# One more weight chunk under the projection, x ahead of the weights, and the last 8 MB in another order

## The chip, the cores and the metric

The kernel runs on one core of a Trainium2 chip. The metric is the device time in microseconds of one execution. Before the change it is 1363.29 us, the median of three runs (1362.73 to 1363.33).

## The reference

One layer on x, 256 rows of 2048 float32:

```
h    = rms_norm(x) ; proj = h @ w_in                    # 2048 x 6736
x   += [sparse attention || retention](proj) @ w_out    # 2048 x 2048
h    = rms_norm(x)
top group of 4, then the top 2 of its 8 experts, gates from a softmax
y    = sum over experts of  gate * ( silu(h @ w1[e]) * (h @ w3[e]) ) @ w2[e]
out  = x + y                                            # w1, w3: 32 x 2048 x 512, w2: 32 x 512 x 2048
```

The attention takes the 64 best keys of a block-causal index score; the retention is a decayed product of queries and keys with a rotation in front. w_in and w_out are 72 MB together, the expert weights 32 x 12 MB, which is 384 MB. Every expert weight is read once.

## The kernel before, in words

**Projection stage.** `w_in` and `w_out` come in 72 loads of up to 1 MB (index `q`) into four raw buffers (`RAW`). Each load holds two units (index `u`, 144 in all); ACT rounds a unit into `w_hi` (L574), DVE takes the rest into `w_lo` (L854), and PE multiplies three times (L1304 to L1306), 12 products of 128x512 to a unit. `SPLIT` is 4: ACT may be four units ahead of PE. At the beginning PE transposes x (`turn_x`, L1266), part by part as its four 512 KB column parts land, and ACT and DVE split the result in two (`round_z`, `rest_z`). PE's program holds all eight `turn_x` before the first unit, and the attention, the retention and the router are put between units at fixed places of each engine's program.

**SyncE's queue.** SP issues in program order x part 0, the identity, the first gain, raw load 0, x parts 1 to 3, then the raw loads. From `q` = 4 on a raw load waits until DVE has finished the units four loads back (`lo_done`). Beside the raw loads 65 to 68 it issues four chunks of expert weights, and after the last raw load the others, as their places come free.

**GpSimd's queue.** It issues the small constants (four gain vectors, the retention gains, the table of positions and cosines) once x is transposed, and, once the retention is done (`ret_ready`), the second norm's gains and the router's weights, seven small transfers. Its own work is the q and k gains, the rotation, and copies of x.

**Expert stage.** Experts go in eight teams of four. A team has 24 chunks of 2 MB: 16 of w1 and w3, 8 of w2 (`TEAM_CHUNKS`). The ring holds `RING` = 8 chunks of 16 KB a partition. The first team has `EXTRA` = 3 more places: the x buffer, once its content is copied away (chunk 8), and two over the buffers of the projection (`spare`, chunks 9 and 10). `first_slot(k)` gives the slot of the first team's chunk k, `first_landed` and `chunk_landed` what to wait for. SP loads chunk k when `ring_used` says that its slot is free; later teams fetch w1 and w3 in loads of 4 MB. PE gathers a team's tokens (L1514), multiplies up (L1559), turns the hidden rows, multiplies down (L1597) and scatters (L1526) into x, where DVE adds. Between the last router logits and the first gather PE waits for the choice of experts (`sel_ready`), which DVE makes.

**The end.** The last team's second half of w2 (rows s = 0 and 1 of each partition, 2048 columns each) comes in three `LAST_PIECES`, each of four transfers (one an expert): row 0 whole (4 MB), row 1's column blocks 0 and 1 (2 MB), row 1's blocks 2 and 3 (2 MB). After each of the two last pieces PE multiplies its blocks (L1649), ACT copies them (L816), PE scatters them (L1661), DVE adds them to x (L1238), and SP stores the output in three parts (L461).

The software DMAs of GpSimd have a reservation of 16 KB a partition in SBUF.

Of the kernel before, what the change touches and what calls it, by code (L numbers as in the profile page):

```python
# [36 lines left out]
P = 128  # L37
SEQ, D = 256, 2048
TH = SEQ // P
C = D // P  # L40
CHUNK = 64
HEADS, HD, KV = 8, 128, 2
# [9 lines left out]
NB = 512  # L52
# [23 lines left out]

RING, EXTRA = 8, 3
UP_CHUNKS, DOWN_CHUNKS = 4 * TEAM, 2 * TEAM
TEAM_CHUNKS = UP_CHUNKS + DOWN_CHUNKS
LAST_GROUP = TEAM_CHUNKS - TEAM  # L80
LAST_PIECES = [(0, 0, 4), (1, 0, 2), (1, 2, 2)]
STORES = [(0, 2), (2, 1), (3, 1)]
# [16 lines left out]
def chunk_slot(k):  # L99

    return k % RING
# [22 lines left out]
def build(nc, x, norm1_g, w_in, q_norm_g, k_norm_g, idx_k_ln_w, idx_k_ln_b, ret_norm_g, w_out,  # L124
          norm2_g, w_group, w_router, w1, w3, w2, consts, out):
    ctx = ExitStack()
    with ctx:
        def sb(name, shape, dt=F32):
            return ctx.enter_context(nc.sbuf_tensor(name, shape, dt))

        def sem(name):
            return ctx.enter_context(nc.semaphore(name))
# [34 lines left out]
        g2_col = sb("g2_col", [P, C])  # L167
        g2_gate = sb("g2_gate", [P, C])
        ps = ctx.enter_context(nc.psum_tensor("ps", [P, 8, 512], F32))

# [10 lines left out]
        xs_flat = xs[:, :, :].rearrange("p t n -> p (t n)")  # L181
        extra = [xs_flat, spare[0], spare[1]]
        zT = half_buf[:, :].rearrange("p (b c t) -> p b c t", b=2, c=4)
# [90 lines left out]
        stored = sem("stored")  # L274
        ring_used = sem("ring_used")
        raw_landed = [sem(f"raw_landed{i}") for i in range(RAW)]
        hi_done, lo_done = sem("hi_done"), sem("lo_done")
# [95 lines left out]
        def _(sp):  # L373
# [36 lines left out]
            for q in range(UNITS // 2):  # L410
                if q == 1:
                    for i in range(1, X_PARTS):
                        load_x(i)
                if q >= RAW:
                    sp.wait_ge(lo_done, 2 * (q - RAW) + 2)
                at = raw_buf[:, q % RAW * 2048:(q % RAW + 1) * 2048]
                if 2 * q >= UNITS_IN:
                    nb, e = OUT_ORDER[2 * q - UNITS_IN]
                    src, c, col, n = w_out_v, 2 * e, nb * NB, NB
                else:  # L420
                    col, n = block_cols(q // 4)
                    src, c = w_in_v, q % 4 * 4
                sp.dma_start(at[:, 0:4 * n].rearrange("p (c n) -> p c n", c=4),
                             src[:, c:c + 4, col:col + n]).then_inc(raw_landed[q % RAW], 16)
# [18 lines left out]
            def last_team(it):  # L443

                matrices(it, TEAMS - 1)
                for k in range(UP_CHUNKS, LAST_GROUP):
                    sp.wait_ge(ring_used, it * TEAM_CHUNKS + (k - RING + 1))
                    load(k, TEAMS - 1)
                for i, (j, n, count) in enumerate(LAST_PIECES):
                    at = j * D + n * NB  # L450
                    for m in range(TEAM):
                        k = LAST_GROUP + m
                        if i == 0:
                            sp.wait_ge(ring_used, it * TEAM_CHUNKS + (k - RING + 1))
                        src = w2_v[(TEAMS - 1) * TEAM + m, 1]
                        sp.dma_start(ring[:, chunk_slot(k), at:at + count * NB],
                                     src[:, at:at + count * NB]).then_inc(piece_in[i], 16)
                for n, count in STORES:
                    sp.wait_ge(added, it * 8 + (16 + TH * (n + count)))
                    cols = slice(n * NB, (n + count) * NB)  # L460
                    sp.dma_start(out_t[:, :, cols], xs[:, :, cols]).then_inc(stored, 16)  # L461

# [35 lines left out]
        def _(pool):  # L498
            pool.wait_ge(z_turned, 8)
            for dst, src in ((gain_q, q_norm_g), (gain_k, k_norm_g), (ln_w, idx_k_ln_w), (ln_b, idx_k_ln_b)):  # L500
                pool.dma_start(dst, src.partition_broadcast(P).rearrange("p l n -> p (l n)")).then_inc(gains_in, 16)
            pool.dma_start(gr_rows[:, :], ret_norm_g.rearrange("l (h d) -> (l h) d", d=HD)).then_inc(ret_gain_in, 16)
            pool.dma_start(const[:, P:CONSTS], consts[:, P:CONSTS]).then_inc(const_in, 16)
            pool.wait_ge(gains_in, 64)
# [8 lines left out]
            for part, blocks in ((RQ, 8), (RK, 10)):  # L513
                pool.wait_ge(evacuated, 2 * blocks)
                for th in range(TH):
# [11 lines left out]
                    pool.wait_ge(rotated, n)  # L527
            pool.wait_ge(ret_ready, 2)
            pool.dma_start(g2_col[:, :], norm2_g.rearrange("l (p c) -> p (l c)", c=C)).then_inc(g2_in, 16)
            pool.dma_start(g2_gate[:, :].rearrange("p (q c) -> p q c", q=4),  # L530
                           norm2_g.rearrange("l (q p c) -> p (l q) c", q=4, c=4)).then_inc(g2_in, 16)
            pool.dma_start(stage_g.rearrange("p (q n) -> p q n", q=4), w_group.rearrange("l (q p c) g -> p (l q) (c g)", q=4, c=4)).then_inc(router_in, 16)
            for g in range(GROUPS):
                pool.dma_start(stage_r[:, g].rearrange("p (q n) -> p q n", q=4),
                               w_router[0, g].rearrange("(q p c) e -> p q (c e)", q=4, c=4)).then_inc(router_in, 16)
            for nb in range(OUT_BLOCKS):
# [11 lines left out]
        def _(act):  # L548
# [21 lines left out]
            def round_unit(u):  # L570
                act.wait_ge(raw_landed[u // 2 % RAW], 16 * (u // 2 // RAW + 1))
# [259 lines left out]
        def _(v):  # L831
# [183 lines left out]
            def router_weights():  # L1015
# [13 lines left out]
                last.then_inc(router_laid, 1)  # L1029

            for u in range(UNITS):
                if u < 8:
                    rest_z(u)
                rest_unit(u)
# [220 lines left out]
        def _(pe):  # L1255
# [379 lines left out]
            def last_team(it):  # L1635
                ups(it)
                pe.wait_ge(added, it * 8 + 16)
                turn_hm(it)
                turn_gate(it)
                pe.wait_ge(hm_T_ready, it + 1)  # L1640
                down(it, (0,))
                pe.wait_ge(gate_T_ready, it + 2)
                for i, (j, n0, count) in enumerate(LAST_PIECES):
                    pe.wait_ge(piece_in[i], 16 * TEAM)
                    for n in range(n0, n0 + count):
                        for m in range(TEAM):
                            part = slice(SLOTS * m, SLOTS * (m + 1))
                            at = j * D + n * NB
                            last = mm(ps[part, 4 + n, :], hm_lhsT(m, 2 + j),  # L1649
                                      ring[:, chunk_slot(LAST_GROUP + m), at:at + NB], start=False, stop=(j == 1))  # L1650
                        if j == 1:
                            last.then_inc(y_whole, 1)
                    if j == 0:
                        continue
                    for n in range(n0, n0 + count):
                        pe.wait_ge(y_ready, it * 4 + (4 + n + 1))
                        for th in range(TH):
                            s = TH * n + th
                            if s >= 2:
                                pe.wait_ge(added, it * 8 + (16 + s - 1))  # L1660
                            mm(ps[:, 3 - s % 2, :], gate_T[:, th * P:(th + 1) * P], y_sb[:, n * NB:(n + 1) * NB],  # L1661
                               start=True, stop=True).then_inc(scattered, 1)

# [49 lines left out]
```

## Time and profile before

| what | value |
|---|---|
| median of three runs | 1363.29 us |
| profiled execution, its own time | 1364.37 us |
| its span | 1362.5 us |
| mean granted TensorE clock | 0.865 |
| PE / DVE / ACT / POOL busy | 72% / 24% / 23% / 6% of the span |
| moved by the DMA engines | 480.69 MB, mean 353 GB/s |

Times inside the profile are microseconds from the start of the span. PE is the matrix engine, PEld its weight load, SPq the issue of DMAs by SP, L and a number a line of the kernel. A row of the timeline has a start, a duration, the engine, the line, the operation and how many are merged. An fp32 product shows as two records.

### The profile page before, as it was taken

To read this page: it belongs to the slowest core of one execution; us is meant where nothing else is said; L and a number is where in the kernel's file an instruction comes from. 1 tells how busy PE (TensorE), PEld (TensorE's weight loads), DVE (VectorE), ACT (ScalarE), POOL (GpSimd) and SP (SyncE) were. 2 spreads that over 40 slices of the span, in tenths; PEclk is the share of its full clock that TensorE was granted. 3 is DMA by queue.
4 is the path that set the end of the run, shared out by engine and by line. 5 is a ranking of instruction groups with operands and counts; after the bars stand their busy time and mean duration, and the time that the engine had idled before them with its cause. 6 is when DMAs were issued, how large, how long until landed. Compare 5 with 4: busy or idle time off the path is not lost.

```text
span 1362.5 us, 18965 instructions
## 1 busy us (share of the span) xinstructions
PE 985.4 (72%) x8264; PEld 654.3 (48%) x8264; DVE 330.6 (24%) x504; ACT 306.6 (23%) x553; POOL 80.0 (6%) x61
## 2 busy tenths in 40 slices
PE   7999999999999875556566365547736563674547
PEld 6987887888888651324234133313413421342222
DVE  5457967544753200010010000001001000100101
ACT  6545555555543310001001000100100010010000
POOL 1000242500110020000000000000000000000000
PEclk9999999999999888778787777888878777986888
DMA  8744644544596999999999999999999999999997
GB/s 278 231 153 158 213 145 137 183 164 147 192 411 237 405 426 435 430 426 431 432 432 425 436 431 427 433 431 433 424 435 432 426 434 432 429 425 435 430 423 305
DMA packets 61412, 480.69 MB, mean 353 GB/s; under 512 B 3816, under 2 KB 8096, under 8 KB 43952
## 3 DMA queue, kind: packets, MB, share of 16 engines
q1 hardware_dynamic: 60832, 478.89, 85.9%
q0 software_dynamic: 528, 1.06, 0.3%
q8 instruction: 38, 0.62, 0.2%
q14 instruction: 14, 0.11, 0.0%
HBM read 477.84 MB, written 2.10 MB: 352 GB/s over the span
## 4 chain that ended last, share of the span: by engine, by line
DMA 48%; PE 47%; DVE 2%; SPq 1%; issue 1%; ACT 1%; ACTq 0%
DMA ring<-w_dram 48%; PE ps L1559 11%; PE ps L1304 9%; PE ps L1306 9%; PE ps L1305 9%; PE ps L1597 5%; DVE w_lo L854 1%; PE ps L1514 1%; PE ps L1320 1%; DMA xs<-x_dram 1%; SPq L393 1%; PE ps L1661 1%; PE ps L1414 0%; PE ps L1336 0%; SPq L400 0%
## 5 line engine op out<-in xcount | busy, mean ns | idle before, releaser
L1559 PE MATMUL ps<-ring,side_buf 128*32 128x256 f32 x4000 | 273.5, 438 | 252.3 <-DMA ring<-w_dram 252.3
L1559 PEld LDWEIGHTS ps<-ring,side_buf 128*32 128x32 f32 x4000 | 155.9, 126 | 372.9 <-issue 316.1
L1304 PE MATMUL ps<-w_hi,zT_half 128*128 128x512 f32 (+2 forms) x576 | 221.7, 385 | 1.7 <-DVE w_lo L854 1.7
L1306 PE MATMUL ps<-w_hi,zT_half 128*128 128x512 f32 (+2 forms) x576 | 218.6, 379 | 0.0
L1305 PE MATMUL ps<-w_lo,zT_half 128*128 128x512 f32 (+2 forms) x576 | 218.5, 379 | 0.0
L854 DVE TENSOR_TENSOR w_lo<-raw_buf,w_hi 128x1024 fp32r<-128x1024 f32 (+2 forms) x144 | 182.0, 1281 | 142.7 <-ACT w_hi L574 142.0
L1597 PE MATMUL ps<-ring,side_buf 128*32 128x512 f32 x960 | 129.6, 701 | 97.5 <-DMA ring<-w_dram 97.2
L574 ACT CAST w_hi<-raw_buf 128x1024 fp32r<-128x1024 f32 (+2 forms) x144 | 143.6, 1016 | 107.5 <-PE ps L1306 101.4
L1230 DVE TENSOR_TENSOR xs<-xs,ps 128x512 f32<-128x512 f32 x56 | 38.5, 688 | 487.8 <-PE ps L1526 487.7
L792 ACT ACTIVATE side_buf<-ps,st 128x256 f32<-128x256 f32 x16 | 6.7, 470 | 554.2 <-PE ps L1559 554.2
L1597 PEld LDWEIGHTS ps<-ring,side_buf 128*32 128x32 f32 x960 | 35.8, 127 | 186.0 <-issue 179.5
L1304 PEld LDWEIGHTS ps<-w_hi,zT_half 128*128 128x128 f32 x576 | 108.2, 188 | 23.3 <-DVE w_lo L854 3.2
L1306 PEld LDWEIGHTS ps<-w_hi,zT_half 128*128 128x128 f32 x576 | 108.1, 188 | 20.5
L1305 PEld LDWEIGHTS ps<-w_lo,zT_half 128*128 128x128 f32 x576 | 108.2, 188 | 19.2
L1218 DVE SCALAR_TENSOR_TENSOR side_buf<-ps,st,side_buf 128x256 f32<-128x256 f32 x16 | 7.0, 479 | 253.4 <-ACT side_buf L792 253.4
L1514 PE MATMUL ps<-const,buf_a 128*128 128x128 f32 x512 | 63.6, 284 | 0.0
L1514 PEld LDWEIGHTS ps<-const,buf_a 128*128 128x128 f32 x512 | 60.4, 197 | 3.6 <-issue 3.3
L809 ACT COPY side_buf<-ps 128x512 f32<-128x512 f32 x28 | 14.4, 600 | 207.2 <-PE ps L1597 207.2
L1526 PE MATMUL ps<-side_buf 128*128 128x512 f32 x112 | 54.0, 618 | 0.0
L765 ACT ACTIVATE side_buf<-ps,g_col 128x128 f32<-128x128 f32 x128 | 36.5, 368 | 36.2 <-PE ps L1514 36.2
L1526 PEld LDWEIGHTS ps<-side_buf 128*128 128x128 f32 x112 | 17.3, 188 | 33.8 <-DVE xs L1230 27.5
L1206 DVE TENSOR_TENSOR const<-route,const 128x256 f32 (+1 forms) x8 | 3.4, 424 | 60.8 <-PE ps L1585 59.9
(192 smaller groups left out, 501.3 us busy)
## 6 DMA issues: line engine op xcount, KB each, us to landing
ring<-w_dram SPq DMA_DIRECT2D x56, 4096.0 KB, 25.1
ring<-w_dram SPq DMA_DIRECT2D x73, 2048.0 KB, 21.4
raw_buf<-w_in_dram SPq DMA_DIRECT2D x48, 1024.0 KB, 5.0
raw_buf<-w_out_dram SPq DMA_DIRECT2D x16, 1024.0 KB, 6.0
spare<-w_dram SPq DMA_DIRECT2D x2, 2048.0 KB, 13.1
ring<-w_dram SPq DMA_DIRECT2D x4, 1024.0 KB, 14.0
ring<-w_dram SPq DMA_DIRECT2D x8, 512.0 KB, 17.4
raw_buf<-w_in_dram SPq DMA_DIRECT2D x4, 608.0 KB, 6.2
```

The lines of the kernel that those rows point to most:

```text
L574: nc.scalar.copy(split(w_hi, u), raw(u)).then_inc(hi_done, 1)
L765: last = nc.scalar.activation(h_e[:, c, :], ps[:, 2 + j % 2, cc * P:(cc + 1) * P], ACT.Copy, scale=g2_col[:, c:c + 1])
L809: nc.scalar.copy(y_sb[:, n * NB:(n + 1) * NB], ps[:, 4 + n, :]).then_inc(y_ready, 1)
L854: V.tensor_tensor(split(w_lo, u), raw(u), split(w_hi, u).bitcast(F32), ALU.subtract).then_inc(lo_done, 1)
L1230: V.tensor_tensor(xo, xo, ps[:, 3 - s % 2, :], ALU.add).then_inc(added, 1)
L1304: mm(b, zhi(c)[:, t], wh, start=(c == 0), stop=False)
L1305: mm(b, zhi(c)[:, t], wl, start=False, stop=False)
L1306: last = mm(b, zlo(c)[:, t], wh, start=False, stop=(c == C - 1))
L1514: last = mm(ps[:, 2 + j % 2, (c % 4) * P:(c % 4 + 1) * P], z[:, th, c * P:(c + 1) * P], pick_p[:, th].rearrange("p e s -> p (e s)"), start ...
L1526: mm(ps[:, 3 - s % 2, :], gate_T[:, th * P:(th + 1) * P], y_sb[:, n * NB:(n + 1) * NB], start=True, stop=True).then_inc(scattered, 1)
L1559: last = mm(ps[part, up, pair * WIDE:(pair + 1) * WIDE], h_e[:, c, slots], w[m][:, cc * NB + h * WIDE:cc * NB + (h + 1) * WIDE], start=(c ...
L1597: last = mm(ps[part, 4 + n, :], hm_lhsT(m, j), w[m][:, j % 2 * D + n * NB:j % 2 * D + (n + 1) * NB], start=(j == 0), stop=(j == J - 1))
```

## The change

`EXTRA` becomes 4. The fourth place is a new buffer `place` of 16 KB a partition; the software DMAs' reservation is set to 128 bytes. The first team's chunk 11 goes there, issued by SP ahead of raw load 40. With `EXTRA` the slots of the first team turn by one: beside the raw loads 65 to 68 go the chunks 4 to 7, afterwards 0, 2, 1 and 3 (before: 5, 6, 7, 0, then 1, 3, 2 and 4).

All transfers that GpSimd issued are SP's: the six constants ahead of raw load 5, and the seven of the router ahead of raw load 63, behind a wait for `ret_ready`. At the start SP issues x parts 1 and 2, then raw load 0's first half with a semaphore of its own, x part 3, and raw load 0's second half. ACT and DVE take their part of x one unit earlier. PE gets three products of 128x512 into an unused bank ahead of the wait for `sel_ready`. The last pieces are: both rows of the column blocks 0 and 1 (4 MB), row 0 of blocks 2 and 3 (2 MB), row 1 of them (2 MB); PE scatters the blocks 0 and 1 after the first piece and the blocks 2 and 3 after the last.

```diff
-RING, EXTRA = 8, 3
+RING, EXTRA = 8, 4
-LAST_PIECES = [(0, 0, 4), (1, 0, 2), (1, 2, 2)]
+LAST_PIECES = [(0, 2, 0, 2), (0, 1, 2, 2), (1, 1, 2, 2)]
+        place = sb("place", [P, 4096])
-        extra = [xs_flat, spare[0], spare[1]]
+        extra = [xs_flat, spare[0], spare[1], place[:, :]]
@@ sync: in the loop over the raw loads q
-                if q == 1:
-                    for i in range(1, X_PARTS):
-                        load_x(i)
+                if q == 5:
+                    for dst, src in ((gain_q, q_norm_g), (gain_k, k_norm_g), (ln_w, idx_k_ln_w), (ln_b, idx_k_ln_b)):
+                        sp.dma_start(dst, src.partition_broadcast(P).rearrange("p l n -> p (l n)")).then_inc(gains_in, 16)
+                    sp.dma_start(gr_rows[:, :], ret_norm_g.rearrange("l (h d) -> (l h) d", d=HD)).then_inc(ret_gain_in, 16)
+                    sp.dma_start(const[:, P:CONSTS], consts[:, P:CONSTS]).then_inc(const_in, 16)
+                if q == 40:
+                    load_first(11)
+                if q == 63:
+                    sp.wait_ge(ret_ready, 2)
+                    sp.dma_start(g2_col[:, :], norm2_g.rearrange("l (p c) -> p (l c)", c=C)).then_inc(g2_in, 16)
+                    sp.dma_start(g2_gate[:, :].rearrange("p (q c) -> p q c", q=4),
+                                 norm2_g.rearrange("l (q p c) -> p (l q) c", q=4, c=4)).then_inc(g2_in, 16)
+                    sp.dma_start(stage_g.rearrange("p (q n) -> p q n", q=4),
+                                 w_group.rearrange("l (q p c) g -> p (l q) (c g)", q=4, c=4)).then_inc(router_in, 16)
+                    for g in range(GROUPS):
+                        sp.dma_start(stage_r[:, g].rearrange("p (q n) -> p q n", q=4),
+                                     w_router[0, g].rearrange("(q p c) e -> p q (c e)", q=4, c=4)).then_inc(router_in, 16)
...
+                if q == 0:
+                    load_x(1)
+                    load_x(2)
+                    sp.dma_start(at[:, 0:2 * n].rearrange("p (c n) -> p c n", c=2),
+                                 src[:, c:c + 2, col:col + n]).then_inc(raw_first, 16)
+                    load_x(3)
+                    sp.dma_start(at[:, 2 * n:4 * n].rearrange("p (c n) -> p c n", c=2),
+                                 src[:, c + 2:c + 4, col:col + n]).then_inc(raw_landed[0], 16)
@@ sync: last_team
-                        src = w2_v[(TEAMS - 1) * TEAM + m, 1]
-                        sp.dma_start(ring[:, chunk_slot(k), at:at + count * NB],
-                                     src[:, at:at + count * NB]).then_inc(piece_in[i], 16)
+                        src = w2_v[(TEAMS - 1) * TEAM + m, 1].rearrange("p (s n) -> p s n", s=2)
+                        dst = ring[:, chunk_slot(k), :].rearrange("p (s n) -> p s n", s=2)
+                        cols = slice(n * NB, (n + count) * NB)
+                        sp.dma_start(dst[:, j:j + rows, cols], src[:, j:j + rows, cols]).then_inc(piece_in[i], 16)
@@ sync: after the raw loads
             sp.wait_ge(lo_done, UNITS - 4)
+            load_first(0)
+            sp.wait_ge(unit_used, UNITS - 4)
+            load_first(2)
+            sp.wait_ge(lo_done, UNITS)
             load_first(1)
-            sp.wait_ge(unit_used, UNITS - 4)
+            sp.wait_ge(unit_used, UNITS)
             load_first(3)
-            sp.wait_ge(lo_done, UNITS)
-            load_first(2)
-            sp.wait_ge(unit_used, UNITS)
-            load_first(4)
             load_first(9)
@@ gpsimd: the same thirteen dma_start lines go, with wait_ge(z_turned, 8) and wait_ge(ret_ready, 2)
@@ scalar (vector has the same with rest_z)
+            round_z(0)
             for u in range(UNITS):
-                if u < 8:
-                    round_z(u)
+                if u < 7:
+                    round_z(u + 1)
                 round_unit(u)
@@ tensor: ahead of the wait for sel_ready
+            for _ in range(3):
+                mm(ps[:, 0, :], ident, const[:, 0:NB], start=True, stop=True)
             pe.wait_ge(sel_ready, 1)
@@ tensor: last_team, after down(it, (0,))
+                piece(0)
+                scatter_block(0)
+                scatter_block(1)
+                piece(1)
+                piece(2)
+                scatter_block(2)
+                scatter_block(3)
@@ build
-    nc = bacc.Bacc("TRN2", target_bir_lowering=False, num_devices=1)
+    nc = bacc.Bacc("TRN2", target_bir_lowering=False, num_devices=1, dynamic_dma_scratch_size=128)
```

## Rows read from the trace of the kernel before

**Rows 1.** The page: DMA rate in 40 equal slices, and the chain by line.
```profile
GB/s 278 231 153 158 213 145 137 183 164 147 192 411 237 405 426 435 430 426 431 432 432 425 436 431 427 433 431 433 424 435 432 426 434 432 429 425 435 430 423 305
DMA ring<-w_dram 48%; PE ps L1559 11%; PE ps L1304 9%; PE ps L1306 9%; PE ps L1305 9%; PE ps L1597 5%; DVE w_lo L854 1%; PE ps L1514 1%; PE ps L1320 1%; DMA xs<-x_dram 1%; SPq L393 1%; PE ps L1661 1%; PE ps L1414 0%; PE ps L1336 0%; SPq L40
```

**Rows 2.** Busy time by stretch: PE, PEld, DVE, ACT, POOL, clock, DMA share, GB/s.
```profile
60.00:443.00 383.00, 381.26 (x1878) 318.61 (x1876) 233.43 (x316) 190.99 (x278) 66.97 (x41) 1.00 0.57 196
...
443.00:1347.00 904.00, 541.27 (x6048) 285.36 (x6048) 63.22 (x139) 80.56 (x219) 9.45 (x10) 0.80 1.00 429
```

**Rows 3.** SP's expert loads between the stages, in order of time.
```profile
420.76 22.54 SPq L393 DMA_DIRECT2D ring<-w_dram  x4
...
461.46 37.27 SPq L393 DMA_DIRECT2D ring<-w_dram  x13
```

**Rows 4.** Issue to landing of the loads issued at 447.2 and 447.5.
```profile
DMA to landing us min/median/max: 14.3/16.5/18.8
```

**Rows 5.** PE on the first team: chunks 2 to 7, and 12 and 13.
```profile
465.69 10.57 PE L1559 MATMUL ps<-ring,side_buf 128*32 128x256 f32 x192
...
482.77 3.84 PE L1559 MATMUL ps<-ring,side_buf 128*32 128x256 f32 x66
```

**Rows 6.** A raw load beside the four early chunks, and PE at that time.
```profile
raw_buf<-w_out_dram SPq DMA_DIRECT2D x1, 1024.0 KB, 15.2
392.00:400.00 8.00, 8.00 (x38) 6.59 (x36) 5.30 (x5) 4.88 (x8) 3.15 (x2) 1.00 1.03 416
```

**Rows 7.** Raw load 0, issued at 2.2 us: size and time to landing.
```profile
raw_buf<-w_in_dram SPq DMA_DIRECT2D x1, 1024.0 KB, 7.1
```

**Rows 8.** The first 20 us, in order of time; idle time in brackets.
```profile
10.64 5.54 PE L1266 MATMUL ps<-const,xs 128*128 128x128 f32 x24 [3.25 <-DMA xs<-x_dram]
12.74 3.21 PEld L1266 LDWEIGHTS ps<-const,xs 128*128 128x128 f32 x16 [0.53 <-DMA xs<-x_dram]
15.95 0.47 PE L1304 MATMUL ps<-w_hi,zT_half 128*128 128x512 f32 x1
16.79 1.05 ACT L574 CAST w_hi<-raw_buf 128x1024 fp32r<-128x1024 f32 x1 [4.01 <-DMA raw_buf<-w_in_dram]
17.87 1.23 DVE L854 TENSOR_TENSOR w_lo<-raw_buf,w_hi 128x1024 fp32r<-128x1024 f32 x1 [3.54 <-ACT w_hi L574]
```

**Rows 9.** GpSimd's router transfers, and DVE around them.
```profile
357.62 2.97 POOL L534 DMA_DIRECT2D half_buf<-w_router_dram  x4
353.76 1.22 DVE L996 TENSOR_TENSOR flat<-flat 128x1024 f32<-128x1024 f32 x1
357.63 1.23 DVE L854 TENSOR_TENSOR w_lo<-raw_buf,w_hi 128x1024 fp32r<-128x1024 f32 x1 [1.48 <-ACT w_hi L574]
```

**Rows 10.** Between the router and the first up product: PE, and the clock.
```profile
450.10 0.69 PE L1497 MATMUL ps<-route,const 128*128 128x64 f32 x2 [2.98 <-DVE route L1153]
452.02 5.79 PE L1514 MATMUL ps<-const,buf_a 128*128 128x128 f32 x32
461.33 2.05 PE L1514 MATMUL ps<-const,buf_a 128*128 128x128 f32 x16
452.00:454.00 2.00, 2.00 (x10) 1.98 (x10) 1.12 (x9) 0.00 (x0) 0.00 (x0) 0.50 1.03 442
```

**Rows 11.** The end: a window of pieces, products, scatters; landing of the transfer issued at 1334.43.
```profile
1338.00:1346.00 8.00, 7.11 (x68) 1.93 (x56) 0.00 (x0) 0.00 (x0) 0.00 (x0) 1.00 1.02 410
...
1342.05 3.64 PE L1649 MATMUL ps<-ring,side_buf 128*32 128x512 f32 x32 [0.58 <-DMA ring<-w_dram]
1347.07 1.92 PE L1649 MATMUL ps<-ring,side_buf 128*32 128x512 f32 x16 [1.39 <-DMA ring<-w_dram]
1348.93 3.95 PE L1661 MATMUL ps<-side_buf 128*128 128x512 f32 x8
1352.81 1.92 PE L1649 MATMUL ps<-ring,side_buf 128*32 128x512 f32 x16
DMA to landing us min/median/max: 17.5/17.5/17.5
```

More of the change, by code:

```diff
@@ L275, in build @@
         ring_used = sem("ring_used")
+        raw_first = sem("raw_first")
         raw_landed = [sem(f"raw_landed{i}") for i in range(RAW)]
@@ L422, in _ @@
                     src, c = w_in_v, q % 4 * 4
-                sp.dma_start(at[:, 0:4 * n].rearrange("p (c n) -> p c n", c=4),
-                             src[:, c:c + 4, col:col + n]).then_inc(raw_landed[q % RAW], 16)
+                if q == 0:
[6 more added lines that the diff above has]
+                                 src[:, c + 2:c + 4, col:col + n]).then_inc(raw_landed[0], 16)
+                else:
+                    sp.dma_start(at[:, 0:4 * n].rearrange("p (c n) -> p c n", c=4),
+                                 src[:, c:c + 4, col:col + n]).then_inc(raw_landed[q % RAW], 16)
                 if q == FLAT_FREE:
@@ L448, in last_team @@
                     load(k, TEAMS - 1)
-                for i, (j, n, count) in enumerate(LAST_PIECES):
-                    at = j * D + n * NB
+                for i, (j, rows, n, count) in enumerate(LAST_PIECES):
                     for m in range(TEAM):
@@ L498, in _ @@
         def _(pool):
[L499 to L503, printed above, removed]
             pool.wait_ge(gains_in, 64)
@@ L527, in _ @@
                     pool.wait_ge(rotated, n)
[L528 to L535, printed above, removed]
             for nb in range(OUT_BLOCKS):
@@ L570, in round_unit @@
             def round_unit(u):
-                act.wait_ge(raw_landed[u // 2 % RAW], 16 * (u // 2 // RAW + 1))
+                if u == 0:
+                    act.wait_ge(raw_first, 16)
+                else:
+                    act.wait_ge(raw_landed[u // 2 % RAW], 16 * (u // 2 // RAW + 1))
                 if u >= SPLIT:
@@ L1029, in router_weights @@
                 last.then_inc(router_laid, 1)
+            rest_z(0)
             for u in range(UNITS):
-                if u < 8:
-                    rest_z(u)
+                if u < 7:
+                    rest_z(u + 1)
                 rest_unit(u)
@@ L1642, in last_team, with piece @@
                 pe.wait_ge(gate_T_ready, it + 2)
-                for i, (j, n0, count) in enumerate(LAST_PIECES):
+                def piece(i):
+                    j0, rows, n0, count = LAST_PIECES[i]
                     pe.wait_ge(piece_in[i], 16 * TEAM)
                     for n in range(n0, n0 + count):
[L1646 to L1651, printed above, removed]
-                            last.then_inc(y_whole, 1)
[L1653 to L1662, printed above, removed]
@@ new lines, in piece @@
+                        for j in range(j0, j0 + rows):
+                            for m in range(TEAM):
+                                part = slice(SLOTS * m, SLOTS * (m + 1))
+                                at = j * D + n * NB
+                                last = mm(ps[part, 4 + n, :], hm_lhsT(m, 2 + j),
+                                          ring[:, chunk_slot(LAST_GROUP + m), at:at + NB], start=False, stop=(j == 1))
+                        if j0 + rows == 2:
+                            last.then_inc(y_whole, 1)
@@ new lines, in scatter_block @@
+                def scatter_block(n):
+                    pe.wait_ge(y_ready, it * 4 + (4 + n + 1))
+                    for th in range(TH):
+                        s = TH * n + th
+                        if s >= 2:
+                            pe.wait_ge(added, it * 8 + (16 + s - 1))
+                        mm(ps[:, 3 - s % 2, :], gate_T[:, th * P:(th + 1) * P], y_sb[:, n * NB:(n + 1) * NB],
+                           start=True, stop=True).then_inc(scattered, 1)
+                piece(0)
```

## The prediction

> **What bounds the kernel now.** I read the page first: 40 slices of DMA rate and the chain [rows 1]. From the 14th slice on (about 443 us) the rate stays between 405 and 437 GB/s up to the last slice, and the largest item of the chain is the ring's weight loads, 48%. So there are two stages. Up to 443 us PE is busy for 381.26 of 383 us from 60 us on, at the full clock, with the DMA engines at 0.57; from 443 to 1347 us the DMA share is 1.00 at 429 GB/s, and PE works 541 of 904 us [rows 2]. PE's 11% at L1559 and the other product lines of the chain in the second stage are steps between two loads and not its limit: the transfer engines have no gap that a faster PE could close. The end of the kernel is therefore (the moment at which the stream starts) + (bytes left then) / (429 GB/s) + (what PE, DVE and the store do behind the last bytes). Each part of the change is priced by which of the three it touches.
>
> When does the stream start? SP's expert loads [rows 3]: four from 420.76 to 443.3, the last of them only when unit 144 is done, then three into the other places up to 447.5. From 443 on something is always queued: the one issued at 447.5 lands at 447.5 + 18.8 = 466.3 us [rows 4], and the next is issued at 461.46 [rows 3].
>
> **Chunk 11 early.** Of 192 chunks, 7 are issued before 443, 185 after it: 185 x 2.097 MB / 429 GB/s = 904 us, which is the stretch of [rows 2]. One chunk less behind 443 is 2.097 MB / 429 GB/s = 4.89 us. Its slot order turns by one, but before 461 the same number of loads waits for the same events (lo_done 140, unit_used 140, lo_done 144, unit_used 144), so the stream neither starts later nor runs dry sooner. Would it run dry later, since chunks 8 to 11 free no slot of the ring when they are used? The chunks 12 to 19 go out as chunks 0 to 7 are used, in the old run by 465.69 + 10.57 = 476.3 us, and last 8 x 4.89 = 39 us from 466, to 505. Chunk 20 needs 12 used, which was so at 482.77 + 3.84 = 486.6 [rows 5]. It doesn't run dry, and I count the whole 4.89. Bounds: 0, if gaps appear that I don't see; 5.2, at 405 GB/s, the slowest full slice of [rows 1]. The transfer itself falls into the first stage, where the DMA share is 0.57 [rows 2]. It puts 4.9 us ahead of a raw load; the four early chunks did the same four times over, a raw load took 15.2 us to land, and PE was busy 8.00 of 8 us [rows 6]. Cost 0; without that cover, 4.9.
>
> The row gives 429 GB/s for this core [rows 2]. The Trainium skill (DMA: Bandwidth & Descriptors, Specifications) states a limit of about 358 GB/s for HBM to one core; by that figure the chunk would be worth 5.86 us and not 4.89. The trace does not agree: 904 us at 429 GB/s.
>
> **x first.** PE's last 16 transposes start when x part 2 lands (12.74) and the first unit follows at 15.95 [rows 8]; raw load 0 landed at 2.2 + 7.1 = 9.3 [rows 7], with 1.5 MB landed by then (x part 0 and itself). I place landings by bytes in SP's order. New order: x parts 0, 1, 2 make 1.5 MB, so part 2 lands near 9.3; the half of raw load 0 near 10.6; x part 3 completes 2.5 MB, as x part 2 did before, so it lands at 12.7; the second half at 14.0; raw load 1 as before. PE then has only 8 transposes left at 12.7. The 16 behind 12.74 end at 10.64 + 5.54 = 16.18, 3.44 us, so 8 take 1.7. The first unit starts about 14.3 to 14.5 instead of 15.95: 1.6 us. Is unit 0 ready? ACT 1.05 and DVE 1.23 behind 10.6, so by 12.9. Unit 2 becomes the tightest: raw load 1 lets ACT start at 16.79, DVE ends at 17.87 + 1.23 = 19.10 [rows 8], and PE wants it two units behind 14.4; a unit is 1.23 + 1.48 = 2.71 us, the distance at which DVE's rests follow when PE sets the pace [rows 9], so at 19.8. 0.7 us are left. Since PE is busy 99.5% of the time from 60 to 443 [rows 2], the shift arrives at the start of the stream whole. I take 1.6, between 0 (raw load 1 late by the four smaller transfers) and 2.4 (landings faster than by bytes).
>
> **Constants by SP.** No row has SP issue these; GpSimd took 2.97 us for four [rows 9], 0.74 each, and I take that as the upper end for SP. The six at q = 5 are then at most 4.5 us of issue, where SP has 5.4 us (two units) from one raw load to the next. They are read from unit 24 on. The seven at q = 63 stand behind `ret_ready`, which DVE gives at 353.76 + 1.22 = 354.98; raw load 63 would go out at 357.63 + 1.23 = 358.86, when unit 119 is done [rows 9]. Between them are 3.9 us for 7 x 0.74 = 5.2 us of issue at most, so raw load 63 goes out at most 1.3 us late, and three raw loads of 5.4 us lie between it and PE. Cost 0, without them 1.3. GpSimd's own sequence gets shorter and is waited for by nobody here.
>
> **Three products ahead of `sel_ready`.** PE stands 2.98 us before 450.10, and the clock is then at its lower level (0.50): 32 records of the gather take 5.79 us against 2.05 for 16 at full clock [rows 10]. Four fp32 products of this shape took 3.95 us with their waits [rows 11], so three take at most 2.96 at the full clock, just the gap. If the clock stays up, the first up product starts 1.7 us earlier. It is worth 0 at the end, because the queue holds work until 466.3 and the first freed slot comes at 461.46; for the same reason a delay would cost 0 up to 4.8 us. If the products ran at the lower clock they would end about 2.9 us late, inside the cover.
>
> **The end.** By bytes the pieces land where they did relative to the stream: 4 MB, 2 MB, 2 MB, at 1342.05, 1347.07 and 1334.43 + 17.5 = 1351.9 [rows 11]. Before, PE was not free for the last one until 1352.81, held by the scatter of blocks 0 and 1 (3.95 us) behind the piece of 1347.07. Now: piece 0 1342.05 to 1345.7, four scatters to 1349.7, piece 1 to 1351.6, and piece 2 starts at its landing, 1352.0. What follows (1.9, 3.95, the last add, the store) is as before. Gain 1352.8 - 1352.0 = 0.8 us. Bounds: 1.6, if the last landing comes earlier; -0.5, if the first piece, now in rows of 4 KB instead of 8 KB, slows by what these rows show: the window in which mostly pieces of 4 KB rows move has 410 GB/s against the stream's 429, 4.4%, which on 4 MB (9.8 us) is 0.4 us.
>
> **The sum.** On the profiled execution: span 1362.5 - 4.89 - 1.6 - 0.8 = 1355.2, with the 1.87 us around the span 1357.1 (it had 1364.37). That execution stood 1.08 above the median, so the forecast is 1363.29 - 7.3 = 1356.0 us.
>
> **The rivals.**
>
> *A: the stream has gaps now, and the chunk is not worth its bytes.* The transition is where they could come, near 443 (idle until unit 144 is done) or 487 to 505. For it: the three extra places free no ring slot, now four. Against: the share of 1.00 over all 904 us and the 18 us of margin above. Only x and the end remain: 1363.3 - 2.4 = 1360.9.
>
> *B: PE starves behind SP's longer queue.* Mechanism: SP issues in order, so raw loads wait behind chunk 11, the seven small transfers or `ret_ready`; each us over the cover is a us of PE. For it: `ret_ready` leaves less than the seven issues may take. Against: three loads of reserve. 2 to 4 us lost: 1358 to 1360. The Trainium skill (DMA: Bandwidth & Descriptors, Queues, rings and completion order) says that each engine takes turns between the rows of different issuers and works one row in ring order. By it the small transfers passed the raw loads on GpSimd's row and now hold them up on SP's; no run here shows that yet.
>
> *C: slower. The stream's rate falls.* Place: 443 to the end. A new 16 KB buffer and a smaller reservation move the tiles in SBUF, and chunk 11 is read from where the software DMAs had their own memory; if the transfer engines take another place less well, every load pays. Price: 904 us, so 1% is 9.0 us; from 0.8% (425.5 GB/s) on it eats all 7.3 us. At 1.3% the time is 1367.7. For it: the slices vary from 405 to 437 [rows 1]. Against: they do so by where a slice cuts, and nothing in the change touches what a load is.
>
> *D: the change doesn't do what it says:* the place is there, but chunk 11 lands at 40 without one load less later. The code has 12 to 23 left for the loop, so I see no way to it. 1358 to 1361.
>
> **How the numbers follow.** Forecast 0.80, A 0.06, B 0.07, C 0.05, D 0.02. The forecast's own range: low 1363.3 - 5.2 - 2.4 - 1.6 = 1354.1, less 0.3 for the spread of the runs, 1353.8; high with nothing from x and the end losing 0.5, 1363.3 - 4.9 + 0.5 = 1358.9, drawn to 1359.4 to take in most of B. This kernel's measurement tells some 0.2% (2.7 us) from no change, so faster means below 1360.6: the forecast 0.80, B but for its far end 0.06, D 0.02, together 0.88. Same: A 0.06 and B's far end 0.01, 0.07. Slower: C, 0.05.
>
> **What would show it.** In the profile after: the first unit at about 14.4 us and no wait of PE for `w_lo` in the next units; loads issued near 441.4 where 443 stood; DMA share 1.00 from there to about 1340.5 instead of 1347 (6.5 us: the chunk and x), over 4.9 us less; the clock at 1.00 through the gather; the last add 7.3 us earlier. Wrong would be: a rate other than 429 by over 1%, a DMA share under 0.95 in any stretch of 8 us behind 445, idle time of PE before L1304 at L574's raw loads, or a last landing that trails piece 2's start.

## The result, and the profile after

The changed kernel takes 1352.06 us (median of four, 1351.20 to 1352.57) against 1363.01 us before (median of four); the ratio is 0.992, 95% interval 0.9907 to 0.9933. That is 10.95 us faster where 7.3 were forecast, and 1.7 us under the lower end of the range. On another chip the same kernel came to 1351.26 against 1363.65, 12.4 us.

The page after, rate by slice, which answers to [rows 1]:

```profile
GB/s 292 243 134 173 200 154 194 185 161 150 184 420 246 388 428 436 433 426 433 434 434 426 437 433 427 437 433 433 427 436 431 431 436 432 431 429 434 432 426 323
```

The slices look alike at first sight; most in the second stage are 1 to 3 GB/s higher. That is where the forecast lost its 4 us, and a slice is too coarse to show it well. The profiled execution of after has a span of 1349.4 us, 13.1 less than before. I cut both at the same events: the first unit's first record, the issue into the spare places when unit 144 is done ("spare issue" below, the start of the stream), PE's start on the second half of w2 of a team (each time behind a wait for the ring), and the start of the last piece's products.

| from | to | before, us | after, us | difference |
|---|---|---|---|---|
| start | first unit | 15.95 | 13.27 | -2.68 |
| first unit | spare issue | 427.39 | 427.39 | 0.00 |
| spare issue | team 0, second half of w2 | 87.23 | 81.43 | -5.80 |
| team 0 | team 6, the same | 702.70 | 699.57 | -3.13 |
| team 6 | last piece | 119.54 | 118.13 | -1.41 |
| last piece | end | 9.69 | 9.61 | -0.08 |

The first stage is the same to 0.01 us, only earlier. The third line holds the chunk (4.85) and 0.95 more; the fourth, in which nothing was edited at all, gives 3.13 us. These are the two ends of that stretch and, between them, the teams 4 and 5, before and then after (start, duration, records, in brackets PE's wait):

```profile
530.57 9.07 PE L1597 MATMUL ps<-ring,side_buf 128*32 128x512 f32 x64 [10.95 <-DMA ring<-w_dram]
...
999.56 8.39 PE L1597 MATMUL ps<-ring,side_buf 128*32 128x512 f32 x64 [12.61 <-DMA ring<-w_dram]
...
1116.42 9.69 PE L1597 MATMUL ps<-ring,side_buf 128*32 128x512 f32 x64 [10.90 <-DMA ring<-w_dram]
...
1233.27 9.29 PE L1597 MATMUL ps<-ring,side_buf 128*32 128x512 f32 x64 [10.89 <-DMA ring<-w_dram]
```

```profile
522.09 8.67 PE L1616 MATMUL ps<-ring,side_buf 128*32 128x512 f32 x64 [9.56 <-DMA ring<-w_dram]
...
988.96 9.04 PE L1616 MATMUL ps<-ring,side_buf 128*32 128x512 f32 x64 [12.20 <-DMA ring<-w_dram]
...
1105.31 8.89 PE L1616 MATMUL ps<-ring,side_buf 128*32 128x512 f32 x64 [12.34 <-DMA ring<-w_dram]
...
1221.66 8.75 PE L1616 MATMUL ps<-ring,side_buf 128*32 128x512 f32 x64 [12.38 <-DMA ring<-w_dram]
```

A team's 24 chunks take 1116.42 - 999.56 = 116.86 us before and 1105.31 - 988.96 = 116.35 after, and so from each team to the next from team 1 on, to 0.02 us (from team 0 to team 1 it is 118.40 and 117.83). PE waits 9.6 us and more ahead of each of these lines, so it is the stream's own period; below, "a team" with a time means this period. It is 0.51 us or 0.44% shorter; over the 904 us of the stream [rows 2] that is 3.9 us.

The beginning after, which answers to [rows 8]:

```profile
7.69 3.68 PE L1283 MATMUL ps<-const,xs 128*128 128x128 f32 x16 [0.64 <-DMA xs<-x_dram]
10.35 1.04 ACT L589 CAST w_hi<-raw_buf 128x1024 fp32r<-128x1024 f32 x1 [2.42 <-DMA raw_buf<-w_in_dram]
11.65 1.90 PE L1283 MATMUL ps<-const,xs 128*128 128x128 f32 x8 [0.29 <-DMA xs<-x_dram]
13.27 0.51 PE L1321 MATMUL ps<-w_hi,zT_half 128*128 128x512 f32 x1
```

x part 3 lands at 11.65, where I had placed it at 12.7 by its bytes; the first unit follows 13.27 - 11.65 = 1.62 us later, where I had put 1.7 for the remaining eight transposes. SP's router transfers, which answer to GpSimd's of [rows 9], and the queue between the stages, to [rows 3, 4]:

```profile
352.32 0.34 SPq L422 DMA_DIRECT2D g_col<-norm_g_dram  x1
352.70 0.44 SPq L423 DMA_DIRECT2D g_gate<-norm_g_dram  x1
353.18 0.51 SPq L425 DMA_DIRECT2D half_buf<-w_group_dram  x1
353.73 3.11 SPq L428 DMA_DIRECT2D half_buf<-w_router_dram  x4
...
440.66 4.93 SPq L395 DMA_DIRECT2D spare<-w_dram  x2
445.63 0.44 SPq L395 DMA_DIRECT2D xs<-w_dram  x1
459.15 29.47 SPq L395 DMA_DIRECT2D ring<-w_dram  x12
```

The seven issues take 356.84 - 352.32 = 4.5 us, within the 5.2 allowed for, and no wait of PE follows. The end, which answers to [rows 11]:

```profile
1333.46 3.95 PE L1682 MATMUL ps<-side_buf 128*128 128x512 f32 x8
1337.35 1.92 PE L1671 MATMUL ps<-ring,side_buf 128*32 128x512 f32 x16
1339.79 1.92 PE L1671 MATMUL ps<-ring,side_buf 128*32 128x512 f32 x16 [0.52 <-DMA ring<-w_dram]
1341.64 3.95 PE L1682 MATMUL ps<-side_buf 128*128 128x512 f32 x8
```

The scatter of blocks 0 and 1 now lies ahead of the two last pieces, and the last one's products wait 0.52 us for their data instead of for PE, as forecast.

### The profile page after: what moved, and what is told of

Same layout as the page of the kernel before. It is cut to its first block, busy times and chain, and to the rows that moved or that the text cites. A ratio compares the mean times of both kernels' runs of the same rounds, so it can differ in the third digit from the quotient of the medians.

```text
span 1349.4 us, 18972 instructions
## 1 busy us (share of the span) xinstructions
PE 989.2 (73%) x8270; PEld 657.5 (49%) x8270; DVE 330.8 (25%) x504; ACT 307.0 (23%) x553; POOL 71.7 (5%) x48
## 4 chain that ended last, share of the span: by engine, by line
PE 48%; DMA 47%; SPq 2%; DVE 1%; issue 1%; ACT 1%; DVEq 0%; ACTq 0%
DMA ring<-w_dram 46%; PE ps L1578 12%; PE ps L1321 9%; PE ps L1323 9%; PE ps L1322 9%; PE ps L1616 5%; SPq L482 1%; DVE w_lo L870 1%; PE ps L1337 1%; SPq L395 1%; DMA xs<-x_dram 1%; PE ps L1431 1%; PE ps L1533 1%; PE ps L1353 0%; PE ps L1514 0%
## 5 line engine op out<-in xcount | busy, mean ns | idle before, releaser
L1616 PE MATMUL ps<-ring,side_buf 128*32 128x512 f32 x960 | 126.4, 686 | 98.1 <-DMA ring<-w_dram 97.2
L551 POOL COPY buf_a<-xs 128x512 f32<-128x512 f32 x8 | 11.5, 1465 | 169.1 <-DVE xs L1029 169.1
```

Of the source, the lines that this page charges most:

```text
L1616: last = mm(ps[part, 4 + n, :], hm_lhsT(m, j), w[m][:, j % 2 * D + n * NB:j % 2 * D + (n + 1) * NB], start=(j == 0), stop=(j == J - 1))
```

## The experiments

What was moved in SBUF, beside the buffers, is where they start. From the allocations, the ring begins at byte 16512 of a partition before, which is 128 over a multiple of 256, and at byte 256 after.

**The kernel before, again, and with everything 128 bytes higher.**

```
# b_again: no edit
# b_shift128
+        sb("pad", [P, 32])
+        base = (nc.sbuf_base + 31) // 32 * 32
         ring = sb("ring", [P, RING, 4096])
```

> The kernel before, unchanged. The forecast was 1356.0 us, the changed kernel took 1352.06. Its first unit starts 2.7 us earlier (forecast 1.6), the end gains 0.9 (forecast 0.8), and the landing that PE waits for moves by another 4.0 us between 511 us and 1312 us: a team's 24 chunks, told by the waits of PE for the ring's loads, take 116.35 us in the changed kernel's trace against 116.87 before. Noise theory: such a difference comes from one execution to another; then this run shows a team's period somewhere else than 116.87 by 0.3 us or more. The other theories (placement of the tiles in SBUF; who issues the DMAs; the fourth place) say 116.8 to 116.9 again. Ratio to before 1.000.

> The kernel before with 128 bytes a partition allocated ahead of the ring, so that every tile lies 128 bytes higher. The ring starts at byte 16512 of a partition before (128 over a multiple of 256) and at 256 in the changed kernel. Placement theory: a team's period falls from 116.87 to 116.35 us and the time by 3 to 4 us, to about 1359.5 to 1360.5. Theories of the issuer and of the fourth place, and noise: 116.87, 1363.0.

b_again: 1364.28 us, ratio 1.0006 (0.9996 to 1.0015), a team 116.86 us. b_shift128: 1359.00 us against 1363.82, ratio 0.9965 (0.9951 to 0.9979), a team 116.35 us. Its lines, of two teams in a row:

```profile
1110.84 9.74 PE L1599 MATMUL ps<-ring,side_buf 128*32 128x512 f32 x64 [10.77 <-DMA ring<-w_dram]
...
1227.19 9.60 PE L1599 MATMUL ps<-ring,side_buf 128*32 128x512 f32 x64 [10.77 <-DMA ring<-w_dram]
```

1227.19 - 1110.84 = 116.35. So an unused tile of 128 bytes ahead of the ring brings the old kernel from 1363.82 to 1359.00 us, 4.8 less. The period accounts for 3.9 of them; the rest lies inside the interval of the ratio. b_again kept its 116.86, so the period doesn't differ by chance from one execution to another.

**The changed kernel with its ring off the boundary.**

```
# a_shift128: two small tiles allocated ahead of the ring instead of behind it
+        g_col = sb("g_col", [P, C])
+        g2_gate = sb("g2_gate", [P, C])
         base = (nc.sbuf_base + 31) // 32 * 32
```

> The changed kernel with two small tiles of 128 bytes together allocated ahead of the ring instead of behind it: the ring starts at 384, 128 over a multiple of 256, as it does before the change. Placement theory: a team's period rises to 116.87 us and the time by 3 to 4 us, to about 1355.5. Issuer, fourth place, noise: 116.35 and 1352.1.

1356.66 us, ratio 0.9951 (0.9935 to 0.9968), and the old period is back:

```profile
1108.77 8.74 PE L1616 MATMUL ps<-ring,side_buf 128*32 128x512 f32 x64 [12.52 <-DMA ring<-w_dram]
...
1225.65 10.03 PE L1616 MATMUL ps<-ring,side_buf 128*32 128x512 f32 x64 [12.51 <-DMA ring<-w_dram]
```

1225.65 - 1108.77 = 116.88. The effect goes both ways: the old kernel's stream got faster by it, the changed kernel's slower.

**Which tile, and which boundary.**

```
# b_behind128: the pad behind the ring, ahead of w_hi, w_lo and all the rest
+        sb("pad", [P, 32])
         side = (nc.sbuf_base + 31) // 32 * 32
# b_shift32: as b_shift128 with sb("pad", [P, 8])
# ring_4096: const_sp (below) with sb("pad", [P, 960]) ahead of the ring
```

> The kernel before with 128 bytes a partition between the ring and the tiles behind it: the ring stays at byte 16512, all others lie 128 higher. If the place of the ring, into which the stream writes, sets the rate: a team's period stays 116.86 us and the time 1363. If the place of the tiles that PE, ACT and DVE read and write beside it does: 116.35 and 1359.

> The kernel before with 32 bytes ahead of the ring: it starts at 16544, 160 over a multiple of 256 and 32 over one of 64. If every start off a multiple of 256 costs the same one piece more a row: 116.86 us a team as before. If finer places cost more (off 64 or 128): above 116.86, 1364 or more.

> const_sp (1358.6 us, ring at byte 256) with the ring moved up to byte 4096. If a start on a multiple of 256 is all that counts: 116.35 us a team and 1358.6 again. If wider multiples count as well: below 116.35, and each 0.1 us a team is 0.8 us of the time.

b_behind128 and b_shift32 ran once each (1372.02 and 1364.41 us) and kept the old period, 116.86 and 116.85 us. A shift by 384 bytes, b_shift384, did not fit into SBUF and gave no result; it was to show whether a multiple of 512 does better than one of 256, which ring_4096 answers. ring_4096: 116.35 us, 1359.18, ratio 0.9964 (0.9952 to 0.9977). So it is the ring's start alone. A multiple of 256 is enough (16640 is none of 512), and one of 128 is not:

| ring starts at | over a multiple of 256 | kernels | a team's 24 chunks |
|---|---|---|---|
| 256 | 0 | after, chunk_only, const_sp, a_no_chunk and six more | 116.35 |
| 4096 | 0 | ring_4096 | 116.35 |
| 16640 | 0 | b_shift128 | 116.35 |
| 384 | 128 | a_shift128 | 116.88 to 116.94 |
| 16512 | 128 | before, b_again, b_behind128 | 116.86 |
| 16544 | 160 | b_shift32 | 116.85 |

The traces also show how the time is lost. Beside PE's waits they hold the records of the DMAs (one row of a transfer each), with their durations. A team's stream is 1024 records of 32 KB (the loads of w1 and w3) and 1024 of 16 KB (w2). Between 650 and 1230 us a record took on average:

| ring over a multiple of 256 | executions | 16 KB record | 32 KB record |
|---|---|---|---|
| 0 | 12 | 611.1 ns | 1213.0 ns |
| 128 or 160 | 6 | 614.8 to 615.0 ns | 1216.9 to 1217.0 ns |

Each record is 3.7 to 4.0 ns longer, whether it carries 16 or 32 KB and whether the ring is 128 or 160 off. With 2048 / 16 = 128 records to an engine, 128 x 3.9 ns = 0.50 us a team: the whole 0.51.

The measured time of b_behind128 was another surprise: 1372.02 us, 8 slower, all of it ahead of the spare issue. I ran it again, and then two shorter distances in the changed kernel.

> The kernel with 128 bytes between the ring and the tiles behind it once more: its only execution so far took 1372.0, with the loads' stream starting 7.9 us late and the products of w_hi, w_lo and x 0.233 us apart instead of 0.227. If that was one execution: 1363.7. If it is the distance between the tiles that these products read (x in the ring's part, the weights behind it): 1372 again. A team's period stays 116.86 by either.

```
# a_behind64: g_col (64 bytes) moved between the ring and side; a_behind32: gr_col (32 bytes)
+        g_col = sb("g_col", [P, C])
         side = (nc.sbuf_base + 31) // 32 * 32
```

> The changed kernel with a tile of 64 bytes between the ring and the tiles behind it: x's halves (in the ring's part) stay, w_hi and w_lo lie 64 bytes further. With 128 bytes the first stage took 7.5 to 8 us more. If only the distance of 128 is bad: first stage and time as in a_again, 1351.3 to 1352. If every distance off a multiple of 256 is: some us slower, up to 1360. If the old distance is itself not the best: faster than 1351. The team's period stays 116.35 us by all.

> The same with 32 bytes. The same three answers: 1351.3 to 1352, slower up to 1360, or below 1351; 116.35 us a team.

b_behind128_again: 1371.05, ratio 1.0054 (1.0037 to 1.0070): no accident. a_behind64: 1354.97, 0.9945 (0.9929 to 0.9962). a_behind32: 1360.75, 0.9978 (0.9969 to 0.9988). The periods stayed 116.86, 116.35 and 116.35. I call what was put between the ring and the tiles behind it the distance. From the first unit to the spare issue the stage takes 427.4 us at distance 0 (before, after, a_again, b_shift128; 427.3 to 427.9 in all 14 such executions), 430.1 with 64, 435.1 with 128 (435.0 in its first run) and 436.1 with 32. Products of b_behind128_again, and of b_again, at the same time of the program (start, duration):

```profile
99.92 0.40 PE L1307 MATMUL ps<-w_hi,zT_half 128*128 128x512 f32 x1
100.16 0.39 PE L1305 MATMUL ps<-w_hi,zT_half 128*128 128x512 f32 x1
100.39 0.39 PE L1306 MATMUL ps<-w_lo,zT_half 128*128 128x512 f32 x1
100.62 0.39 PE L1307 MATMUL ps<-w_hi,zT_half 128*128 128x512 f32 x1
100.85 0.39 PE L1305 MATMUL ps<-w_hi,zT_half 128*128 128x512 f32 x1
```

```profile
99.97 0.39 PE L1305 MATMUL ps<-w_lo,zT_half 128*128 128x512 f32 x1
100.19 0.39 PE L1306 MATMUL ps<-w_hi,zT_half 128*128 128x512 f32 x1
100.42 0.39 PE L1304 MATMUL ps<-w_hi,zT_half 128*128 128x512 f32 x1
100.64 0.39 PE L1305 MATMUL ps<-w_lo,zT_half 128*128 128x512 f32 x1
100.87 0.39 PE L1306 MATMUL ps<-w_hi,zT_half 128*128 128x512 f32 x1
```

(100.85 - 99.92) / 4 = 0.233 us from start to start against (100.87 - 99.97) / 4 = 0.225, at a granted clock of 1.00 in both. Over the 80 us from 120 to 200 us the median distance from start to start is 0.227 us at distance 0, 0.229 at 64, 0.232 at 128 and 0.234 at 32. x's halves and the raw buffers lie in the ring's part, w_hi and w_lo behind it; all tiles behind the ring moved together, so which pair does it, and how, stays open. Where the tiles behind the ring start by themselves is not it: they lie 128 over a multiple of 256 in before and on one in after, with the same 427.39 us, and on one in b_behind128. Both kernels of this case had the distance 0, and no part of the result comes from it.

**The parts of the change by themselves.**

```
# const_sp: before + constants and router transfers by SP + reservation of 128 bytes; EXTRA = 3, no place
# chunk_only: const_sp + EXTRA = 4, place, load_first(11) at q == 40, the new slot order
# a_no_chunk: after without place, with the old slot order, and with
-RING, EXTRA = 8, 4
+RING, EXTRA = 8, 3
-                if q == 40:
-                    load_first(11)
...
```

> The kernel before with the constants issued by SP and the reservation of 128 bytes, and nothing else: three places, no chunk 11. Its ring starts at 256. If the constants cost and bring nothing, as I forecast, it equals the kernel before with the ring moved by 128 bytes, 1359.0 us and 116.35 a team. If GpSimd's software DMAs or their issue had a price of their own it is faster than that. And chunk_only, which took 1354.5, would then be 4.9 below it: the chunk by itself.

> The change without x first, without the three products and with the old last pieces: what is left is the fourth place with chunk 11 and the new slot order, the small reservation, and the constants issued by SP. My forecast for this part was 4.89 us: 1358.1. If whatever raises the stream's rate is in it (placement, issuer, fourth place), the time is 1363.0 - 4.9 - 2 to 4, so 1354 to 1356, with a period of 116.35. If the rate came from x first or the end's order, or was noise, 1358.1 with 116.87.

> The changed kernel without the fourth place: three places, no chunk 11, the old slot order; the ring still starts at byte 256. Chunk worth its bytes as forecast: 4.85 us (116.35 / 24) above the changed kernel's 1351.3 to 1352.1, so 1356 to 1357, with 116.35 us a team. If the changed kernel's extra gain hung on the fourth place and not on the ring's start: 1359 or more.

const_sp: 1358.61 us, ratio 0.9960 (0.9947 to 0.9972). b_shift128, which has the ring's place and nothing else, has 0.9965 (0.9951 to 0.9979): the constants, the reservation and the end of the software DMAs bring and cost nothing that shows, as far as the intervals tell (some 2.5 us). chunk_only: 1354.50, 0.9926 (0.9910 to 0.9943). a_no_chunk: 1356.91, 0.9957 (0.9940 to 0.9973), in the range expected. The chunk's price is sharper in the traces. From the spare issue (440.23) to team 0's second half of w2 (526.57) a_no_chunk takes 86.34 us, a_again 522.15 - 440.61 = 81.54: 4.80 us. Between const_sp and chunk_only the same stretch gives 86.80 - 81.69 = 5.11.

```
# a_no_x_first: after with the old order at the start
+                if q == 1:
+                    for i in range(1, X_PARTS):
+                        load_x(i)
...
-                if q == 0:
-                    load_x(1)
-                    load_x(2)
...
-            round_z(0)
...
-                if u < 7:
-                    round_z(u + 1)
+                if u < 8:
+                    round_z(u)
...
# a_old_end: after with the old LAST_PIECES and the scatters inside their loop
-LAST_PIECES = [(0, 2, 0, 2), (0, 1, 2, 2), (1, 1, 2, 2)]
+LAST_PIECES = [(0, 0, 4), (1, 0, 2), (1, 2, 2)]
# a_no_products
-            for _ in range(3):
-                mm(ps[:, 0, :], ident, const[:, 0:NB], start=True, stop=True)
```

> The changed kernel, unchanged, beside its three reduced forms on the same chip. 1352 to 1353; ratio to before 0.992; 116.35 us a team; first unit at 13.3 us.

> The changed kernel with the old order at the start: raw load 0 whole and ahead of x parts 1 to 3, and x's parts split as before. The changed trace has the first unit 2.68 us earlier than the old one, where I forecast 1.6. If the shift reaches the end whole (the stream starts when unit 144 is done): 2.7 us slower than a_again, 1355, and the first unit at about 15.9. If part of it was the constants' new place or an execution's luck: the difference is 1.6 or less.

> The changed kernel with the old last pieces and the old order of the scatters. Forecast 0.8 us slower than a_again, 1353; the last piece's products start 0.8 us later relative to the last landing. If the new order were hidden: no difference.

> The changed kernel without the three products ahead of the wait for sel_ready. Forecast: no difference in time, since the queue holds loads until about 464 us in both; the gather's 32 records at 5.8 us again, and the first load that waits for PE some 2 us nearer to the end of the queue. If the products feed the stream: slower by up to 2 us.

These four were measured on one chip, before at 1363.65. a_again: 1351.26, 0.9912 (0.9898 to 0.9925). a_no_x_first: 1353.16, 0.9922 (0.9908 to 0.9935), 1.9 us more; its first unit starts at 15.73 against 13.18, 2.55 later, and its spare issue 2.53 later. The intervals of the two overlap, so the traces must carry this one. Over all of them, the first unit starts at 15.74 us on average in the ten executions with the old order and at 13.39 in the eight with the new one, 2.35 earlier. a_old_end: 1352.36, 0.9917 (0.9903 to 0.9930), 1.1 us more, of which the trace gives 0.65 to the end (from team 6's second half of w2 to the last piece 1341.65 - 1222.88 = 118.77, against 1339.83 - 1221.71 = 118.12). The five executions with the ring at a multiple of 256 and the old pieces have 118.76 to 118.82 there, the seven with the new ones 118.12 to 118.21. The two profiled executions differ by 1.8 us in all; the other 1.13 is the first unit, later by that much in a_old_end with the same order at the start. The intervals of the two kernels overlap, so this term too stands on the traces. a_no_products: 1351.21, 0.9910 (0.9895 to 0.9925), no difference. The gather of a_no_products, as in [rows 10], and then of a_again:

```profile
447.38 0.69 PE L1514 MATMUL ps<-route,const 128*128 128x64 f32 x2 [2.99 <-DVE route L1170]
...
449.30 5.35 PE L1531 MATMUL ps<-const,buf_a 128*128 128x128 f32 x32
```

```profile
444.22 2.82 PE L1514 MATMUL ps<-const 128*128 128x512 f32 x6
447.38 0.43 PE L1516 MATMUL ps<-route,const 128*128 128x64 f32 x2 [0.34 <-DVE route L1170]
...
448.86 3.84 PE L1533 MATMUL ps<-const,buf_a 128*128 128x128 f32 x32 [0.41 <-DVE const L1186]
```

The granted clock over the 32 gather records is 0.70 in a_no_products (0.50 in the 2.2 us ahead of them, after PE's wait of 2.99 us) and 1.00 in a_again. The three products fit into that wait, the gather falls from 5.35 to 3.84 us, and SP issues its next load at 456.35 instead of 458.31. Nothing of it reaches the end, since transfers were queued until about 463 us in both.

## Why the prediction was too small

**What held.** The end of the kernel is the stream's start, plus the bytes left at the stream's rate, plus the tail; the first stage is PE's. The cut of the two traces has no gap in the stream and nothing lost between the stages.

**The step that failed: the stream's rate.** The term "(bytes left then) / (429 GB/s)" took the rate as the same before and after, and the sum has nothing for a change of it. But the rate hangs on the kernel too: the ring's start went from 128 over a multiple of 256 bytes onto one, through the smaller reservation ahead of it, and the rate rose by 0.44%, 3.9 us. Rival C had the mechanism, "A new 16 KB buffer and a smaller reservation move the tiles in SBUF", and gave it one direction only, slower; no row excluded a gain. Its picture of the memory was off as well: by the allocations it is the ring's first place that now lies over the old reservation (bytes 128 to 16512), not chunk 11's. Its price, 9.0 us for 1%, holds for the measured 0.44% with the other sign. The sign of being wrong that the prediction set for the rate, over 1% from 429, was wider than the 0.44% that moved the time by 3.9 us, more than half of the 7.3 forecast. (The highest full slice of [rows 1] is 436, not 437 GB/s; nothing hangs on it.) With 4 us on the other side of the sum, the forecast would have been 1352.0. The measured time without the shift (a_shift128, 1356.66) lies 0.7 us from the forecast of 1356.0; that it is so near is in part luck, since the terms below miss in both directions.

The Trainium skill (DMA: Bandwidth & Descriptors, How a descriptor splits into AXI transactions) says that a descriptor which does not start on a multiple of 256 bytes begins with a transaction at the boundary below, and that the bytes before its start are fetched unused and still cost. The trace agrees in the boundary, and in that the cost is one fixed piece per record. For the size it does not agree with a simple count: if a record is one descriptor, an estimate from the page is one transaction more in 128 or 64, 1.0% over a team, and 0.44% was measured. Counted in the page's beats of 32 bytes the estimate is 0.52% at 128 over and 0.65% at 160 over, but 160 over took no more than 128 (116.85 and 116.86 us). Why the piece costs 3.9 ns is open. The page's rule was there before the prediction, and I had weighed its bandwidth figure and not this one.

**Chunk 11.** Forecast 4.89 us, measured 4.80 and 5.11 between two pairs of traces. It loaded at 206 us beside the projection and landed in 9.7 us; the stage kept its length to 0.01 us, so the cover held.

**x first.** Forecast 1.6 us, range 0 to 2.4; 1.9 in time, 2.55 between two traces, 2.35 over all of them. The mechanism was right and the landings were off: by bytes x part 3 was due at 12.7 and came at 11.65. The first unit's start scatters from one execution to the next, from 14.09 to 16.31 with the old order and from 12.90 to 14.31 with the new one in kernels with the same order of loads there, and I sized the term on one execution at 15.95.

**The end.** Forecast 0.8, in the trace 0.65.

**Constants, products, rivals.** Both edits forecast at 0 are at 0 in const_sp and a_no_products, as far as their intervals tell. B (PE starved by SP's longer queue) did not happen: from 20 to 440 us PE has the same four idle times over 0.1 us before and after, none over 0.74 us. D did not: the chunk is worth 4.80. Of A (gaps) there is one mark by the prediction's own sign, a stretch of 8 us with a DMA share under 0.95: 942 to 950 us after has 0.94. The stretches on both sides have 1.02 and 1.01, and the period over it is 116.34 us, so it is where the window cuts and no gap.

**The sum as measured:** 4.8 (chunk) + 3.9 (the ring's start) + 1.9 to 2.5 (x) + 0.65 (end) = 11.3 to 11.9 us, between the 10.95 and the 12.4 that the two comparisons gave. The range failed since its lower end stacked three bounds and left the fourth term without one.

## What to carry to other kernels

Where a long stream of DMAs sets the end, its rate is a term of the sum with bounds on both sides, and anything that moves the destination in SBUF (a new tile, a resized reservation, an order of allocation) touches it: look at the start address before and after. Try the tiles that a stream fills on multiples of 256 bytes; in this kernel one unused tile of 128 bytes did it, and took 3.9 to 4.8 us off. Measure a rate by the period between equal events, where 0.4% is plain, not by slices or one window, and look at the mean duration of records of one size: it tells a fixed cost per record from a lower rate; and when a tile is moved for one reason, keep its distance to the tiles that the same products read.

## What the runs showed of the hardware that was not expected

- The transfers' period depends on where their destination starts, to 0.02 us in 116: 116.35 us for 24 chunks of 2 MB at multiples of 256 bytes, 116.85 to 116.94 at 128 and 160 over. The cost is fixed, some 3.9 ns a record, for records of 16 and of 32 KB alike.
- The first stage's products slow down by the distance between tiles: 427.4 us at distance 0, 430.1 at 64, 435.1 at 128, 436.1 at 32, with the same instructions, the full granted clock and no wait added. Its cause was not found.
- The landing of the first transfers differs by up to 2.2 us between executions with the same order of loads (first unit at 14.09 to 16.31 us), and passes on to the stream's start, since the first stage between keeps its 427.4 us.
